# Attention scores of two layers as two stacked fp32r passes instead of one fp32 product

## The chip, the cores and the metric

The kernel runs on one NeuronCore of a Trainium2 chip. The metric is the time of one execution on the device, in microseconds; the lower the better. Before the change three runs took 4530.76, 4531.95 and 4536.92 us, median 4531.95 us. TensorE (PE) multiplies matrices, its weight loads have a row of their own (PEld); VectorE is DVE, ScalarE is ACT, GpSimd is POOL, and SP only issues DMAs.

## What is computed

One sequence of 512 tokens, width 1024, goes through two layers (a feed-forward block, a mixer of a linear recurrence and an attention with a forgetting gate, a second feed-forward block) and then through a second model part with its own mixer, memory attention and an expert layer. The change lies in the attention of the two layers:

```python
def forgetting_attention(q, k, v, f_logit, g_q, g_k):
    qn = rms_norm(q, g_q).transpose(0, 2, 1, 3)
    kn = rms_norm(k, g_k).transpose(0, 2, 1, 3)
    cum = jnp.cumsum(jax.nn.log_sigmoid(f_logit), axis=1).transpose(0, 2, 1)
    for blk in range(seq // Q_BLOCK):
        s = jnp.einsum("bhqd,bhkd->bhqk", qn[:, :, q0:q1], kn[:, :, :q1]) * HEAD_DIM ** -0.5
        s = s + cum[:, :, q0:q1, None] - cum[:, :, None, :q1]
        s = jnp.where(mask, s, -jnp.inf)
        p = jax.nn.softmax(s, axis=-1)
        outs.append(jnp.einsum("bhqk,bhkd->bhqd", p, vh[:, :, :q1]))
```

There are 16 heads of 64 features and 4 query blocks of 128 tokens; the mask is causal. Everything is float32.

## The kernel before

Features lie on the 128 partitions, tokens along the free dimension. Every weight comes as a tile of 128 x 2048 floats. ScalarE copies it to fp32r (`WH`, line 166, two halves), VectorE subtracts to get the rest (`WL`, line 174, two halves), and TensorE makes each product of three fp32r passes: high by high, high by low, low by high (`mm3`, lines 193 to 195). In what follows this is the weight split: `act_next` and `dve_next` split the tile after next.

The attention of a layer works through 8 pairs of heads. One head of a pair is on partitions 0 to 63, the other on 64 to 127. In `pe_attention` the work of three pairs is interleaved on TensorE, in an order written out by hand. While the eight steps of pair i run (2 heads by 4 query blocks, the score of block qb having 128 x (qb + 1) columns), parts of the projection of pair i + 2 fill in (`beside`); after them comes the rest of that projection (16 groups of three passes in all), and in its middle the sums, the spread and the turn for the head norm of pair i + 1 and for the output of pair i. Ahead of the last two groups stand the first two scores of pair i + 1 (`first_scores`).

A step goes: TensorE makes the score in a PSUM bank (line 1231 in plain fp32, and line 1233, which adds the causal mask by an fp32r matmul); VectorE takes the maximum (line 1035, `top`); ScalarE takes the exponential and the row sum (line 1087) and releases `p_ready`; TensorE turns the result by 128 x 128 transposes (line 993, the turn); VectorE copies that to SBUF (line 1047, `copy`); TensorE multiplies by the values (line 1003). There are three score banks, so the fourth score waits for the first exponential.

The score matmul has all 128 rows in use though a head has 64 features: `QZ[hh]` holds the normed Q of its head on its own 64 partitions, and on the other 64 the running sum of the forget gate (from `CQ`) masked by `HMASK`; `KZ[hh]` holds the normed K and there ones or the negative sums. In this way one product gives the score with both gate terms.

Between two pairs ScalarE's queue is: roots and the exponential's table, two copies of the spread norm factors (`widen`, line 1356), the high part of pair i's output (`outputs`, YH, line 1368), the weight split (line 166). VectorE's queue is: the mask products (line 1421), four norm instructions of 64 rows (two for Q, line 1425, two for K, line 1429), the low part of the output (line 1448), the weight split (line 174), and then the maxima of the next pair. The queues of an engine run strictly in program order, and every wait is on a semaphore.

Once per layer, before the attention, `dve_forget_sums` (line 1193) makes the running sums of the gate and fills `CQ` and the fixed rows of `KZ`.

Of the kernel before, what the change touches and what calls it, by code (L numbers as in the profile page):

```python
# [5 lines left out]
F32 = mybir.dt.float32  # L6
F32R = mybir.dt.float32r
# [6 lines left out]
P = 128  # L14
# [163 lines left out]
def act_next(c, act, tile, halves=(0, 1)):  # L178
    act_split(c, act, tile.t + 1, tile.next_p, tile.next_loads, halves)
# [916 lines left out]

PAIRS = HEADS // 2
JS = [(hh, qb) for hh in range(2) for qb in range(QB)]

# [93 lines left out]
def dve_forget_sums(c, dve, l):  # L1193

    V = c.nc.vector
    F = c.FW
    V.scalar_tensor_tensor(out=F[:, 0, :], in0=F[:, 4, :], scalar=-2.0, in1=F[:, 0, :], op0=ALU.mult, op1=ALU.add)
    V.memset(F[:, 2, :], 1.0)
    V.memset(c.CQ[:, :], 1.0)
    V.memset(c.KZ[0][:, :], 1.0)  # L1200
    V.memset(c.KZ[1][:, :], 1.0)
    dve.drain()
    V.tensor_tensor_scan(F[:, 1, :], F[:, 2, :], F[:, 0, :], 0.0, ALU.mult, ALU.add)
    dve.drain()
    for r in (32, 96):
        V.tensor_copy(c.CQ[r:r + 32, :], F[r:r + 32, 1, :])
    V.tensor_scalar(c.KZ[1][0:32, :], F[0:32, 1, :], -1.0, None, ALU.mult)
    V.tensor_scalar(c.KZ[0][64:96, :], F[64:96, 1, :], -1.0, None, ALU.mult)
    dve.drain()
# [14 lines left out]
def pe_attention(c, pe, cur, l):  # L1224
    base = l * PAIRS

    def steps(i, b):
        def step(hh, qb):
            def scores(S):
                nk = P * qb + P  # L1230
                c.nc.tensor.matmul(S[:, :nk], c.QZ[hh][:, qb * P:qb * P + P], c.KZ[hh][:, :nk],  # L1231
                                   start=True, stop=False)
                return c.nc.tensor.matmul(S[:, nk - P:nk], c.IDR[:, :], c.CAUSALR[:, :], start=False, stop=True)
            return {"nk": P * qb + P, "scores": scores,
                    "values": lambda kb: c.V[:, kb, bass.ds(i * P + hh * HD, HD)],
                    "out": c.PB[:, b, qb * P + hh * HD:qb * P + hh * HD + HD]}
        return Steps((base + i) * 8, [step(*x) for x in JS], (c.PM, c.PT, c.SUM), None, score_banks(b))

# [101 lines left out]
def act_attention(c, act, cur, l):  # L1340
# [25 lines left out]
    def outputs(i):  # L1366
        act.wait_ge(c.sem("ot_ready"), base + i + 1)
        c.nc.scalar.activation(c.YH[:, i, :], c.PB[:, 4, :], ACT.Copy).then_inc(c.sem("ot_hi"), 1)

    def beside(tile):  # L1370
        def work(j):
            if j == 3:
                squares(tile)
        return work
# [4 lines left out]
    exp_table()  # L1379
    widen(0)  # L1380
    act_next(c, act, Tile(cur, 0, 1, 1))
# [11 lines left out]
    exp_table()  # L1393
    widen(i + 1)
    outputs(i)
    act_next(c, act, gate)
    attend(i + 1, last.b, None)
# [8 lines left out]
def dve_attention(c, dve, cur, l):  # L1406
# [3 lines left out]
    def scale(i):  # L1410
# [4 lines left out]
                      c.R16[:, :].unsqueeze(2).to_broadcast([P, 16, HD])).then_inc(c.sem("qk_scale"), 1)  # L1415

    def norm(i, b):
        own, other = [slice(hh * HD, hh * HD + HD) for hh in range(2)], [slice(HD, P), slice(0, HD)]
        col = PRM["g_k"][0]
        for hh in range(2):  # L1420
            V.tensor_scalar(c.QZ[hh][other[hh], :], c.CQ[other[hh], :], c.HMASK[other[hh], bass.ds(i * 2 + hh, 1)],
                            None, ALU.mult)
        dve.wait_ge(c.sem("qk_wide"), (base + i) * 2 + 1)
        for hh in range(2):
            V.scalar_tensor_tensor(out=c.QZ[hh][own[hh], :], in0=c.PB[own[hh], b, :], scalar=c.GQ8[own[hh], l, 0:1],
                                   in1=c.SQ2[own[hh], 0, :], op0=ALU.mult, op1=ALU.mult)
        dve.wait_ge(c.sem("qk_wide"), (base + i) * 2 + 2)
        for hh in range(2):
            last = V.scalar_tensor_tensor(out=c.KZ[hh][own[hh], :], in0=c.PB[own[hh], b + 1, :],
                                          scalar=c.PR[own[hh], l, col:col + 1],  # L1430
                                          in1=c.SQ2[own[hh], 1, :], op0=ALU.mult, op1=ALU.mult)
        last.then_inc(c.sem("qk_ready"), 1)

# [19 lines left out]
    scale(0)  # L1453
    norm(0, first.b)
    dve_next(c, dve, Tile(cur, 0, 1, 1))
# [8 lines left out]
    norm(i + 1, last.b)  # L1464
    outputs(i)
    dve_next(c, dve, gate)
    attend(i + 1, last.b, False)
# [9 lines left out]
CONSTS = {}  # L1477
for _n, _w in (("ident", 128), ("ones", 128), ("ones_head", 128), ("causal", 128), ("head_mask", 16)):
    CONSTS[_n] = (sum(w for _, w in CONSTS.values()), _w)
# [3 lines left out]
def constants():  # L1483

    t = np.zeros((P, NCONST), np.float32)

    def put(name, a):
        at, w = CONSTS[name]
        t[:, at:at + w] = a
    i = np.arange(P)  # L1490
    put("ident", np.eye(P))
    put("ones", 1.0)
    put("ones_head", (i[:, None] // HD == i[None, :] // HD))
    put("causal", np.where(i[None, :] <= i[:, None], 0.0, NEG))
    put("head_mask", (i[:, None] % 32 == np.arange(16)[None, :]))
    return t


def allocate(c):
# [12 lines left out]
    with ExitStack() as s:  # L1512
# [4 lines left out]
    c.CT = c.sb("CT", [P, NCONST])  # L1517
    c.IDENT, c.ONES, c.ONESB, c.CAUSAL, c.HMASK = (
        c.CT[:, CONSTS[n][0]:sum(CONSTS[n])] for n in ("ident", "ones", "ones_head", "causal", "head_mask"))
    c.EPSC = c.sb("EPSC", [P, 1])  # L1520
# [6 lines left out]
    c.LW, c.RT = c.sb("LW", [P, 5, DC]), c.sb("RT", [P, QB])  # L1527
    c.sb("ALIGN", [P, 14])

# [8 lines left out]
    with ExitStack() as y:  # L1538
# [10 lines left out]
        with ExitStack() as s:  # L1549
            c.V = c.sb("V", [P, QB, D], F32, s)  # L1550
            c.CQ = c.sb("CQ", [P, S], F32, s)
            c.KZ = [c.sb(f"KZ{i}", [P, S], F32, s) for i in range(2)]
            with ExitStack() as f:
                c.FW = c.sb("FW", [P, 5, S], F32, f)
            c.QZ = [c.sb(f"QZ{i}", [P, S], F32, s) for i in range(2)]
            c.SQ2 = c.sb("SQ2", [P, 2, S], F32, s)
            c.PM, c.PT = c.sb("PM", [P, 3, S], F32, s), c.sb("PT", [P, 2, S], F32, s)
            c.OQ = c.sb("OQ", [P, QB, P], F32, s)
            c.R16, c.EXPD = c.sb("R16", [P, 16], F32, s), c.sb("EXPD", [P, 1], F32, s)
            c.RE = c.sb("RE", [P, 2, QB, P], F32, s)  # L1560
    allocate2_arena(c, stage)

# [424 lines left out]
def act_proj2(c, act, cur):  # L1987
# [18 lines left out]
    for tile in tiles(act, cur, 1):  # L2006
        act_next(c, act, tile)
        act.wait_ge(c.sem("tile_done"), tile.t + 3)
        A.activation(c.KVC[:, :, :S], c.PB[:, tile.b:tile.b + 2, :], ACT.Copy).then_inc(c.sem("ps_done"), 1)
        act.drain()  # L2010
        act.wait_ge(c.sem("kvc_pad"), 1)
        A.activation(c.KCH[:, :, :], c.KVC[:, :, :], ACT.Copy).then_inc(c.sem("cmp_hi"), 1)
# [55 lines left out]
def dve_angles(c, dve):  # L2068
    V = c.nc.vector
    T = c.T2  # L2070
    dve.wait_ge(c.sem("pos_loaded"), 16)
    V.tensor_copy(T[:, 0, :], T[:, 3, :].bitcast(I32))
# [23 lines left out]
def dve_proj2(c, dve, cur):  # L2096
# [415 lines left out]
def act_mem_raw(c, act):  # L2512

    act.wait_ge(c.sem("mem_loaded"), 16)
    act_raw(c, act, V2 + 1, c.NORM_MEM, c.MEMX, lambda k: p2(c, "memkv_g", k, 1), c.XHM, width=MEM, fresh=False)
# [897 lines left out]
def pool_second(c, pool, d):  # L3413

    pool_sum(c, pool, V2, c.NORM_MIX2, order=DOWN_ORDER)
    pool.wait_ge(c.sem("x_new"), V2 * DC + DC)
    pool.dma_start(c.T2[:, 3, :].bitcast(I32), d["positions"]).then_inc(c.sem("pos_loaded"), 16)
    pool.wait_ge(c.sem("tile_done"), T_GATES2 + 3)
# [4 lines left out]
    pool.wait_ge(c.sem("phase_done"), (PH2 + 1) * 3)  # L3423
    pool.dma_start(c.MEMX[:, :, :], d["mem"]).then_inc(c.sem("mem_loaded"), 16)
    pool_sum(c, pool, V2 + 1, c.NORM_MEM, MEM)
# [83 lines left out]
def layer_tiles(a, l):  # L3509
# [13 lines left out]
    f4 = np.zeros((D, P), f.dtype)  # L3523
    for r in (0, 32, 64, 96):
        f4[:, r:r + HEADS] = f
# [21 lines left out]
def layer_params(a, l):  # L3547
    f4 = np.zeros((P, 1), np.float32)
    for r in (0, 32, 64, 96):
        f4[r:r + HEADS, 0] = a["b_forget"][l]  # L3550
# [104 lines left out]
```

## Time and profile before

| | |
|---|---|
| median of three runs | 4531.95 us |
| profiled execution | 4530.32 us |
| its span, first to last instruction | 4528.5 us |
| TensorE busy | 4418.6 us, 98% |
| weight loads busy | 3702.0 us, 82% |
| VectorE busy | 2733.0 us, 60% |
| ScalarE busy | 1742.6 us, 38% |
| GpSimd busy | 720.8 us, 16% |
| TensorE's share of the chain that ended last | 87% |
| mean granted TensorE clock | 0.991 |

The profile is one execution. Busy time is the union of an engine's instructions; the ends of matmuls are modelled, so the distance from one start (or one weight load) to the next tells more than a duration. Attention of the first layer lies at about 636 to 860 us of the span, that of the second at about 1944 to 2170 us. A half clock means that TensorE was granted 0.50 of its full clock.

### The profile page before, as it was taken

Reading aid. Unit: us, or ns where it says so; the run is one execution under the profiler, and the core shown is the slowest. Engines: PE = TensorE matmul, PEld = TensorE weight load, DVE = VectorE, ACT = ScalarE, POOL = GpSimd, SP = SyncE. Lnnn points to the kernel's source line nnn. Section 1 sums busy time; section 2 is a strip of 40 time slices with the busy share of each in tenths; the row PEclk is TensorE's granted clock in tenths of the full one; section 3 lists DMA queues with packets and bytes.
Section 4 is the critical chain, followed back from the end, with each engine's and each line's share of the span. In section 5 each row is a group of like instructions: output and inputs, shape, how many; then the busy total and the mean of one; then the engine's idle time right before and its main releaser. Section 6 shows DMA issues by size and latency. Waiting matters only on the chain.

```text
span 4528.5 us, 61846 instructions
## 1 busy us (share of the span) xinstructions
PE 4418.6 (98%) x21997; PEld 3702.0 (82%) x21997; DVE 2733.0 (60%) x4435; ACT 1742.6 (38%) x2871; POOL 720.8 (16%) x767
## 2 busy tenths in 40 slices
PE   8999999999999999999999998899999899999999
PEld 7888888888888887888888886687667788888888
DVE  5436556454444436656454278754898877777777
ACT  3223634332232225444332233442226644444444
POOL 0000000000000000000000000010486634333332
PEclk9999999999999999999999998999999999999999
DMA  3222221122222222211222222031224688888887
GB/s 130 100 97 87 95 84 37 66 98 97 101 95 93 102 91 86 103 50 43 93 93 98 97 94 77 1 131 56 82 86 156 266 298 299 304 295 299 299 304 262
DMA packets 91046, 605.13 MB, mean 134 GB/s; under 512 B 12832, under 2 KB 13216, under 8 KB 24288
## 3 DMA queue, kind: packets, MB, share of 16 engines
q1 hardware_dynamic: 58464, 412.95, 24.8%
q0 software_dynamic: 31232, 162.29, 10.4%
q10 hardware_dynamic: 1152, 27.26, 1.4%
q8 instruction: 122, 2.00, 0.2%
q14 instruction: 76, 0.62, 0.0%
HBM read 573.10 MB, written 29.36 MB: 133 GB/s over the span
## 4 chain that ended last, share of the span: by engine, by line
PE 87%; DVE 4%; ACT 2%; issue 2%; DVEq 2%; DMA 1%; POOLq 1%; ACTq 0%; POOL 0%; SPq 0%
PE PB L193 25%; PE PB L195 24%; PE PB L194 24%; PE PB L2741 3%; PE PB L1003 2%; PE PB L1231 2%; PE PB L3030 2%; PE PB L993 1%; PE PB L3045 1%; ACT WH L3196 1%; PE PB L1244 1%; PE PB L2254 1%; POOLq L256 1%; DVE WL L3247 1%; DVE YG L3234 0%
## 5 line engine op out<-in xcount | busy, mean ns | idle before, releaser
L193 PE MATMUL PB<-XH,WH 128*128 128x512 f32 (+1 forms) x3288 | 1260.1, 383 | 21.1 <-DVE WL L174 13.6
L195 PE MATMUL PB<-XH,WL 128*128 128x512 f32 (+1 forms) x3288 | 1242.2, 378 | 0.0
L194 PE MATMUL PB<-XL,WH 128*128 128x512 f32 (+1 forms) x3288 | 1241.2, 378 | 0.0
L174 DVE TENSOR_TENSOR WL<-RAW,WH 128x1024 fp32r<-128x1024 f32 x520 | 637.3, 1267 | 480.4 <-ACT WH L166 458.7
L193 PEld LDWEIGHTS PB<-XH,WH 128*128 128x128 f32 x3288 | 619.4, 188 | 130.3 <-issue 20.9
L194 PEld LDWEIGHTS PB<-XL,WH 128*128 128x128 f32 x3288 | 619.4, 188 | 100.1 <-issue 2.2
L166 ACT ACTIVATE WH<-RAW 128x1024 fp32r<-128x1024 f32 x504 | 504.4, 1049 | 509.8 <-PE PB L195 481.7
L195 PEld LDWEIGHTS PB<-XH,WL 128*128 128x128 f32 x3288 | 618.4, 188 | 100.2
L254 POOL TENSOR_TENSOR SQ<-SQ 128x512 f32<-128x512 f32 x49 | 72.5, 1480 | 2567.8 <-ACT SQ L236 2546.1
L3247 DVE TENSOR_TENSOR WL<-RAW,WH 128x1024 fp32r<-128x1024 f32 x220 | 269.8, 1226 | 220.2 <-ACT WH L3196 219.8
L193 PE MATMUL PB<-WH,WGH 128*128 128x512 f32 x768 | 301.0, 392 | 8.4 <-DVE WGL L3263 8.4
L195 PE MATMUL PB<-WH,WGL 128*128 128x512 f32 x768 | 301.5, 393 | 0.0
L194 PE MATMUL PB<-WL,WGH 128*128 128x512 f32 x768 | 301.0, 392 | 0.0
L525 DVE TENSOR_TENSOR PB<-PB,RBF 128x512 f32<-128x512 f32 x88 | 61.6, 700 | 368.6 <-PE PB L195 368.0
L195 PE MATMUL PB<-HH,WL 128*128 (+1 forms) x704 | 273.9, 389 | 0.0
L193 PE MATMUL PB<-HH,WH 128*128 (+1 forms) x704 | 273.9, 389 | 0.0
L194 PE MATMUL PB<-HL,WH 128*128 (+1 forms) x704 | 273.9, 389 | 0.0
L501 ACT ACTIVATE SIL<-PB 128x512 f32<-128x512 f32 x88 | 52.7, 599 | 562.9 <-DVE PB L525 562.9
L3196 ACT ACTIVATE WH<-RAW 128x1024 fp32r<-128x1024 f32 x220 | 230.9, 1050 | 63.0 <-PE PB L195 60.5
L1087 ACT ACTIVATE PM<-PB,NM 128x128 f32<-128x128 f32 (+2 forms) x208 | 108.6, 523 | 245.9 <-DVE NM L1035 245.5
L193 PEld LDWEIGHTS PB<-WH,WGH 128*128 128x128 f32 x768 | 144.6, 188 | 42.8 <-issue 15.3
L3350 POOL DMA_DIRECT2D GM<-gate_matrix x128 | 114.9, 898 | 401.1 <-DVE WG L3259 371.6
(423 smaller groups left out, 7257.5 us busy)
## 6 DMA issues: line engine op xcount, KB each, us to landing
RAW<-weights SPq DMA_DIRECT2D x381, 1024.0 KB, 4.8
gate_matrix<-STG ACTq DMA_DIRECT2D x5, 4096.0 KB, 12.3
GM<-gate_matrix POOLq DMA_DIRECT2D x128, 160.0 KB, 3.3
RAW<-weights SPq DMA_DIRECT2D x12, 512.0 KB, 3.9
gate_matrix<-STG ACTq DMA_DIRECT2D x2, 2048.0 KB, 7.5
GM<-gate_matrix POOLq DMA_DIRECT2D x128, 32.0 KB, 3.7
X<-x SPq DMA_DIRECT2D x4, 512.0 KB, 8.0
x_home<-X ACTq DMA_DIRECT2D x1, 2048.0 KB, 6.9
```

The costliest lines, as they stand in the source:

```text
L166: c.nc.scalar.activation(c.WH[p][:, cols], c.RAW[p][:, cols], ACT.Copy).then_inc(c.sem("w_hi"), 1)
L174: c.nc.vector.tensor_tensor(c.WL[p][:, cols], c.RAW[p][:, cols], c.WH[p][:, cols].bitcast(F32), ALU.subtract).then_inc(c.sem("w_split"), 1)
L193: c.nc.tensor.matmul(out, wh, xh, start=start, stop=False)
L194: c.nc.tensor.matmul(out, wh, xl, start=False, stop=False)
L195: return c.nc.tensor.matmul(out, wl, xh, start=False, stop=stop)
L1003: last = c.nc.tensor.matmul(step["out"](kb) if merged else step["out"], st.PT[:w, j % 2, kb * P:kb * P + P], step["values"](kb), start=mer ...
L1087: c.nc.scalar.activation(st.PM[:, m, :nk], c.PB[:, st.banks[m], :nk], ACT.Exp, bias=c.NM[:, m:m + 1], scale=1.0, accum_out=st.SUM[:, st.su ...
L1231: c.nc.tensor.matmul(S[:, :nk], c.QZ[hh][:, qb * P:qb * P + P], c.KZ[hh][:, :nk], start=True, stop=False)
L2741: last = c.nc.tensor.matmul(c.PB[:, 6 + half, :DENSE], U[:, k, :], c.NORM_PEER.SQ[:, k, :DENSE], start=k == 0, stop=k == DC - 1)
L3196: A.activation(c.WH[p][:, cols], c.RAW[p][:, cols], ACT.Copy).then_inc(c.sem(f"h{half}_hi"), 1)
L3247: V.tensor_tensor(c.WL[p][:, cols], c.RAW[p][:, cols], c.WH[p][:, cols].bitcast(F32), ALU.subtract)\
L3350: pool.dma_start(c.GM[s][:, :whole].rearrange("p (b t) -> p b t", b=BLOCKS - 1), gm[:BLOCKS - 1, :, expert:expert + 1, :].rearrange("b p e ...
```

## The change

The product of Q and K is made of fp32r passes. The normed Q and K of a pair are first written whole to `QKN` (VectorE, two instructions of 128 rows). `QA[hh]` holds the high part of Q on the head's own 64 partitions and the low part on the other 64; `KA[hh]` holds the high part of K on both halves. Their product is Q's high plus low parts by K's high part. `QB[hh]` holds Q's high part and, on the other 64 partitions, the masked gate sums; `KB[hh]` holds the low part of K, and there the ones and negative sums. The score is then QA by KA, QB by KB, and the causal matmul. The gate sums are themselves split in a high and a low part, on alternate groups of 16 partitions (`halves`).

ScalarE makes the high parts (`high`, four copies of 64 x 512 for each head), VectorE the low ones (`low`, two subtractions for each head). Head 0's stand ahead of `outputs`, head 1's behind it, and both ahead of the weight split. The wait for `qk_ready` moves into the score, once for each head, and `qk_high` is waited for there too. The other edits are SBUF layout, constants, the gate column repeated every 16 rather than every 32 partitions, and some semaphores of the second part that are merged or dropped.

```diff
@@ dve_forget_sums
     V.memset(c.CQ[:, :], 1.0)
-    V.memset(c.KZ[0][:, :], 1.0)
-    V.memset(c.KZ[1][:, :], 1.0)
     dve.drain()
     V.tensor_tensor_scan(F[:, 1, :], F[:, 2, :], F[:, 0, :], 0.0, ALU.mult, ALU.add)
+    for hh in range(2):
+        V.tensor_copy(c.KB[hh][:, :], F[:, 2, :])
+    dve.drain()
+    V.tensor_copy(F[:, 0, :].bitcast(F32R), F[:, 1, :])
+    dve.drain()
+    V.tensor_tensor(F[:, 3, :], F[:, 1, :], F[:, 0, :], ALU.subtract)
+    dve.drain()
+    V.tensor_scalar(F[:, 3, :], F[:, 3, :], c.HALVES[:, 1:2], None, ALU.mult)
+    dve.drain()
+    V.scalar_tensor_tensor(out=F[:, 1, :], in0=F[:, 0, :], scalar=c.HALVES[:, 0:1], in1=F[:, 3, :],
+                           op0=ALU.mult, op1=ALU.add)
     dve.drain()
@@ pe_attention, scores
                 nk = P * qb + P
-                c.nc.tensor.matmul(S[:, :nk], c.QZ[hh][:, qb * P:qb * P + P], c.KZ[hh][:, :nk],
+                if qb == 0:
+                    pe.wait_ge(c.sem("qk_ready"), (base + i) * 2 + (hh + 1))
+                    pe.wait_ge(c.sem("qk_high"), (base + i) * 6 + (hh * 3 + 3))
+                c.nc.tensor.matmul(S[:, :nk], c.QA[hh][:, qb * P:qb * P + P], c.KA[hh][:, :nk],
                                    start=True, stop=False)
+                c.nc.tensor.matmul(S[:, :nk], c.QB[hh][:, qb * P:qb * P + P], c.KB[hh][:, :nk],
+                                   start=False, stop=False)
                 return c.nc.tensor.matmul(S[:, nk - P:nk], c.IDR[:, :], c.CAUSALR[:, :], start=False, stop=True)
@@ first_scores
-        pe.wait_ge(c.sem("qk_ready"), base + i + 1)
@@ act_attention
+    def high(i, hh):
+
+        if hh == 0:
+            act.wait_ge(c.sem("qk_natural"), (base + i) * 2 + 1)
+        c.nc.scalar.activation(c.QA[hh][mine[hh], :], c.QKN[mine[hh], 0, :], ACT.Copy).then_inc(c.sem("qk_high"), 1)
+        c.nc.scalar.activation(c.QB[hh][mine[hh], :], c.QKN[mine[hh], 0, :], ACT.Copy)
+        if hh == 0:
+            act.wait_ge(c.sem("qk_natural"), (base + i) * 2 + 2)
+        for rows in (mine[hh], other[hh]):
+            c.nc.scalar.activation(c.KA[hh][rows, :], c.QKN[mine[hh], 1, :], ACT.Copy).then_inc(c.sem("qk_high"), 1)
...
         widen(i + 1)
+        high(i + 1, 0)
         outputs(i)
+        high(i + 1, 1)
         act_next(c, act, ahead)
@@ dve_attention
+        for g, gain in enumerate((c.GQ8[:, l, 0:1], c.PR[:, l, col:col + 1])):
+            dve.wait_ge(c.sem("qk_wide"), (base + i) * 2 + (g + 1))
+            V.scalar_tensor_tensor(out=c.QKN[:, g, :], in0=c.PB[:, b + g, :], scalar=gain, in1=c.SQ2[:, g, :],
+                                   op0=ALU.mult, op1=ALU.mult).then_inc(c.sem("qk_natural"), 1)
+        dve.drain()
+
+    def low(i, hh):
+
+        dve.wait_ge(c.sem("qk_high"), (base + i) * 6 + (hh * 3 + 1))
+        V.tensor_tensor(c.QA[hh][other[hh], :], c.QKN[mine[hh], 0, :], c.QA[hh][mine[hh], :].bitcast(F32), ALU.subtract)
+        dve.wait_ge(c.sem("qk_high"), (base + i) * 6 + (hh * 3 + 2))
+        V.tensor_tensor(c.KB[hh][mine[hh], :], c.QKN[mine[hh], 1, :], c.KA[hh][mine[hh], :].bitcast(F32), ALU.subtract)\
+            .then_inc(c.sem("qk_ready"), 1)
...
         attend(i, own.b)
         norm(i + 1, after.b)
+        low(i + 1, 0)
         outputs(i)
+        low(i + 1, 1)
         dve_next(c, dve, ahead)
```

For the first pair of a layer there is no output to make; `high(0, 0)`, `high(0, 1)` and `low(0, 0)`, `low(0, 1)` stand between the norm and the weight split.

## Rows read from the trace of the kernel before

**Rows 1.** The page: busy us, share of the span and instructions of each engine.

```profile
PE 4418.6 (98%) x21997; PEld 3702.0 (82%) x21997; DVE 2733.0 (60%) x4435; ACT 1742.6 (38%) x2871; POOL 720.8 (16%) x767
```

**Rows 2.** Timeline (start us, length us, engine, line, operation), weight loads of scores.

```profile
781.40 0.30 PEld L1231 LDWEIGHTS PB<-KZ,QZ 128*128 128x128 f32 x2
...
782.38 0.20 PEld L993 LDWEIGHTS PB<-CT,PM 128*128 128x128 f32 x2 [0.24 <-issue]
...
648.06 0.32 PEld L1231 LDWEIGHTS PB<-KZ,QZ 128*128 128x128 f32 x2
648.30 0.19 PEld L1233 LDWEIGHTS PB<-CAUSALR,IDR 128*128 128x128 f32 x1
648.41 0.30 PEld L1231 LDWEIGHTS PB<-KZ,QZ 128*128 128x128 f32 x2
...
648.95 0.19 PEld L193 LDWEIGHTS PB<-XH,WH 128*128 128x128 f32 x1
```

**Rows 3.** Timeline, neighbouring fp32r passes of 512 and of 256 columns.

```profile
777.99 0.39 PE L194 MATMUL PB<-XL,WH 128*128 128x512 f32 x1
778.22 0.39 PE L195 MATMUL PB<-XH,WL 128*128 128x512 f32 x1
...
377.15 0.28 PE L193 MATMUL PB<-WH,XH 128*128 128x256 f32 x1
377.27 0.28 PE L194 MATMUL PB<-WL,XH 128*128 128x256 f32 x1
```

**Rows 4.** Timeline of one boundary between pairs: ScalarE, VectorE, and the turn.

```profile
772.03 1.09 ACT L1356 ACTIVATE SQ<-PB 128x512 f32<-128x512 f32 x2 [3.27 <-PE PB L1254]
773.76 2.00 ACT L166 ACTIVATE WH<-RAW 128x1024 fp32r<-128x1024 f32 x2
...
772.66 1.52 DVE L1425 SCALAR_TENSOR_TENSOR QZ<-PB,GQ,SQ 64x512 f32<-64x512 f32 x2 [0.55 <-ACT SQ L1356]
776.35 2.35 DVE L174 TENSOR_TENSOR WL<-RAW,WH 128x1024 fp32r<-128x1024 f32 x2
778.92 0.29 DVE L1035 TENSOR_REDUCE NM<-PB 128x1 f32<-128x128 f32 x1 [0.23 <-PE PB L1233]
...
781.34 0.14 PEld L993 LDWEIGHTS PB<-CT,PM 128*128 128x128 f32 x1
```

**Rows 5.** An SBUF copy with its follower (timeline); 512-column subtractions (groups by form).

```profile
106.98 0.63 ACT L503 ACTIVATE HH<-PROD 128x512 f32 x1 [1.01 <-DVE PROD L529]
107.51 1.99 ACT L166 ACTIVATE WH<-RAW 128x1024 fp32r<-128x1024 f32 x2
...
L531 DVE TENSOR_TENSOR HL<-PROD,HH 128x512 f32 x80 | 55.4, 693 | 74.6 <-ACT HH L503 74.6
```

**Rows 6.** Timeline, pair 0 of the first layer: split, first exponential, first turn.

```profile
645.22 2.01 ACT L166 ACTIVATE WH<-RAW 128x1024 fp32r<-128x1024 f32 x2
...
650.68 0.37 ACT L1087 ACTIVATE PM<-PB,NM 128x128 f32<-128x128 f32 x1 [3.45 <-DVE NM L1035]
...
651.26 0.14 PEld L993 LDWEIGHTS PB<-CT,PM 128*128 128x128 f32 x1 [0.30 <-issue]
```

**Rows 7.** Timeline, VectorE behind the forget sums of the first layer.

```profile
613.72 1.22 DVE L890 TENSOR_TENSOR M<-PB,AA 128x1024 f32<-128x1024 f32 x1 [1.54 <-PE PB L195]
```

**Rows 8.** TensorE gaps (timeline); stretches behind them: busy us, third-last granted clock.

```profile
464.91 0.50 PE L193 MATMUL PB<-YH,WH 128*128 128x512 f32 x1 [2.80 <-ACT PB L681]
465.80:469.20 3.40, 3.40 (x10) 2.62 (x9) 1.38 (x2) 1.45 (x3) 0.00 (x0) 0.50 0.63 265
...
2822.25 0.66 PE L993 MATMUL PB<-CT,PM 128*128 128x128 f32 x4 [1.36 <-ACT PM L1087]
2824.40:2831.20 6.80, 6.80 (x25) 5.28 (x25) 5.88 (x14) 1.26 (x5) 0.00 (x0) 0.50 0.00 0
...
2807.58 0.66 PE L993 MATMUL PB<-CT,PM 128*128 128x128 f32 x4 [1.56 <-ACT PM L1087]
2807.50:2811.00 3.50, 3.42 (x26) 2.94 (x26) 3.01 (x8) 1.08 (x4) 0.00 (x0) 1.00 0.00 0
```

More of the change, by code:

```diff
@@ L1380, in act_attention @@
     widen(0)
+    for hh in range(2):
+        high(0, hh)
     act_next(c, act, Tile(cur, 0, 1, 1))
@@ L1415, in scale @@
                       c.R16[:, :].unsqueeze(2).to_broadcast([P, 16, HD])).then_inc(c.sem("qk_scale"), 1)
+    mine, other = HALF_ROWS, HALF_ROWS[::-1]
     def norm(i, b):
-        own, other = [slice(hh * HD, hh * HD + HD) for hh in range(2)], [slice(HD, P), slice(0, HD)]
         col = PRM["g_k"][0]
         for hh in range(2):
-            V.tensor_scalar(c.QZ[hh][other[hh], :], c.CQ[other[hh], :], c.HMASK[other[hh], bass.ds(i * 2 + hh, 1)],
+            V.tensor_scalar(c.QB[hh][other[hh], :], c.CQ[other[hh], :], c.HMASK[other[hh], bass.ds(i * 2 + hh, 1)],
                             None, ALU.mult)
[L1423 to L1432, printed above, removed]
+        for g, gain in enumerate((c.GQ8[:, l, 0:1], c.PR[:, l, col:col + 1])):
[9 more added lines that the diff above has]
+            .then_inc(c.sem("qk_ready"), 1)
     def attend(i, b, ahead=True):
@@ L1454, in dve_attention @@
     norm(0, first.b)
+    for hh in range(2):
+        low(0, hh)
     dve_next(c, dve, Tile(cur, 0, 1, 1))
@@ L1464, in dve_attention @@
     norm(i + 1, last.b)
+    low(i + 1, 0)
     outputs(i)
+    low(i + 1, 1)
     dve_next(c, dve, gate)
@@ L1477 @@
 CONSTS = {}
-for _n, _w in (("ident", 128), ("ones", 128), ("ones_head", 128), ("causal", 128), ("head_mask", 16)):
+for _n, _w in (("ident", 128), ("ones", 128), ("ones_head", 128), ("causal", 128), ("head_mask", 16), ("halves", 2)):
     CONSTS[_n] = (sum(w for _, w in CONSTS.values()), _w)
@@ L1494, in constants @@
     put("causal", np.where(i[None, :] <= i[:, None], 0.0, NEG))
-    put("head_mask", (i[:, None] % 32 == np.arange(16)[None, :]))
+    put("head_mask", (i[:, None] % HEADS == np.arange(HEADS)[None, :]))
+    put("halves", (i[:, None] // HEADS % 2 == np.arange(2)[None, :]))
     return t
@@ L1517, in allocate @@
     c.CT = c.sb("CT", [P, NCONST])
-    c.IDENT, c.ONES, c.ONESB, c.CAUSAL, c.HMASK = (
-        c.CT[:, CONSTS[n][0]:sum(CONSTS[n])] for n in ("ident", "ones", "ones_head", "causal", "head_mask"))
+    c.IDENT, c.ONES, c.ONESB, c.CAUSAL, c.HMASK, c.HALVES = (
+        c.CT[:, CONSTS[n][0]:sum(CONSTS[n])] for n in ("ident", "ones", "ones_head", "causal", "head_mask", "halves"))
     c.EPSC = c.sb("EPSC", [P, 1])
@@ L1551, in allocate @@
             c.CQ = c.sb("CQ", [P, S], F32, s)
[L1552 removed]
+            c.KB = [c.sb(f"KB{i}", [P, S], F32R, s) for i in range(2)]
             with ExitStack() as f:
                 c.FW = c.sb("FW", [P, 5, S], F32, f)
[L1555 removed]
+            c.PM, c.PT = c.sb("PM", [P, 3, S], F32, s), c.sb("PT", [P, 2, S], F32, s)
+            c.QA, c.KA, c.QB = ([c.sb(f"{n}{i}", [P, S], F32R, s) for i in range(2)] for n in ("QA", "KA", "QB"))
             c.SQ2 = c.sb("SQ2", [P, 2, S], F32, s)
[L1557 removed]
             c.OQ = c.sb("OQ", [P, QB, P], F32, s)
@@ L1560, in allocate @@
             c.RE = c.sb("RE", [P, 2, QB, P], F32, s)
+            c.QKN = c.RE[:, :, :, :].rearrange("p g q d -> p g (q d)")
     allocate2_arena(c, stage)
@@ L3523, in layer_tiles @@
     f4 = np.zeros((D, P), f.dtype)
-    for r in (0, 32, 64, 96):
+    for r in range(0, P, HEADS):
         f4[:, r:r + HEADS] = f
@@ L3548, in layer_params @@
     f4 = np.zeros((P, 1), np.float32)
-    for r in (0, 32, 64, 96):
+    for r in range(0, P, HEADS):
         f4[r:r + HEADS, 0] = a["b_forget"][l]
```

21 lines of the change are left out of this document (12 added, 9 removed).

## The prediction

> **What bounds the kernel now.** I read the page's busy shares first: TensorE is busy for 98% of the span and no other engine is above 60% [rows 1]. A microsecond of matmul work removed is then a microsecond of span, provided that TensorE doesn't end up waiting for somebody in its place. So the question is where, in the stage that the change touches, the three engines meet. That stage is the attention of both layers, 16 pairs of heads in all. The first turn of pair 0 starts at 651.26 [rows 6], that of pair 5 at 781.34 [rows 4]: 26.0 us a pair. The second view is the timeline of that boundary between two pairs [rows 4]: the reader is to see that VectorE does the second half of its weight split, and immediately after it the first maximum of the next pair (778.92, after a wait of 0.23 us for the scores). VectorE is thus at that place already as late as it may be, while ScalarE is done with its split at 775.76 (773.76 + 2.00). TensorE reaches the first turn of the new pair (the transposes of line 993) at 781.34 and isn't held there.
>
> **What the faster scores give.** Of TensorE I count from weight load to weight load, since ends of matmuls are modelled. A 512-column score in plain fp32, with its causal matmul, holds TensorE from 781.40 to 782.38, 0.98 us; a 256-column one from 648.41 to 648.95, 0.54 us; a 128-column one from 648.06 to 648.41, 0.35 us [rows 2]. In fp32r one 512-column pass takes 0.23 us and one of 256 columns 0.12 us, start to start [rows 3]; a load whose matmul is short costs 0.11 us (648.30 to 648.41) [rows 2]. The new score is two such passes and the causal one: 2 x 0.23 + 0.11 = 0.57 us at 512 columns, 2 x 0.12 + 0.11 = 0.35 at 256, and three loads, 0.33, at 128. The gains are 0.41, 0.19 and nothing; the 384-column score lies between, 0.30. A head gains 0.90 us, a pair 1.80, the 16 pairs **28.8 us**.
>
> **What is put on ScalarE and VectorE.** Per pair, ScalarE gets eight copies of 64 x 512. The nearest row is a copy from SBUF to fp32r of 512 columns: 0.63 us long, the next instruction 0.53 us after its start [rows 5]. I charge 0.53, since 64 partitions rather than 128 gain nothing in the old norm (0.76 us for each 64-row instruction, 1.52 for two [rows 4]). Bounds: 0.50 (the two PSUM copies at 772.03, 1.09 us together with the last one's tail) and 0.57. VectorE loses two of its four norm instructions (the two new ones do 128 rows each, 0.75 us) and gets four subtractions of 0.69 us [rows 5].
>
> **The boundary walked with these.** All times are those of rows 4.
> - Copies to SQ2 start at 772.03; the norm of Q at 772.66, so QKN's Q is there at 773.41 and its K at 774.17.
> - ScalarE, from 773.45: four copies to 775.57, then YH (0.50) to 776.07, four copies to 778.19. Only now the weight split, which before began at 773.76: 4.4 us later.
> - VectorE's own four subtractions fit in the gaps between these copies, and the low part of head 0 is ready at about 775.9 (KA's first copy ends 775.14, then 0.69), before TensorE wants it at 778.22. So the first scores don't wait.
> - ScalarE's first split half ends at about 779.24 (half of 2.00 us and some tail); VectorE's two halves take 2.35 us from 779.28, to 781.63. Behind them are queued, on VectorE, the maxima of the next pair: 781.66 to 781.95. ScalarE's exponential waits for the maximum, TensorE's turn for the exponential. From the exponential's start to the load of the turn it took 0.58 us in the pair where TensorE was waiting for it (650.68 to 651.26) [rows 6]. So the turn starts at 781.95 + 0.04 + 0.58 = 782.57, against 781.34 before: **1.23 us later**.
> - The scores before the turn gave 0.19 + 0.30, so TensorE stands for 1.23 + 0.49 = 1.7 us there. The scores after it (512, 128, 256, 384, 512 columns) still give 1.31. The pair's net is 1.23 - 1.31 = -0.08 us.
>
> That holds for 14 of the 16 pairs: **-1.1 us**. The gain of 28.8 us is, almost to the last microsecond, spent in a new wait. I find no second new wait in the eight steps: maxima and exponentials start as soon as their scores are there, and these come earlier by as much as TensorE does.
>
> **The first pair of each layer** has no YH, but its copies for both heads stand ahead of the split. ScalarE was free for the split at 645.22 [rows 6]. By the same offsets (773.45 is 0.43 after ScalarE's widening copies leave it free) the copies run from 645.65 to 649.89, the splits of VectorE from 650.98 to 653.33, the maximum to 653.65, the turn starts at 654.27. It was 651.26, so 3.01 us later, with 1.31 given back: +1.7 us, twice: **+3.4 us**. TensorE stands there for about 3.5 us. A gap of 2.80 us (464.91) was followed by 3.4 us at half clock (granted 0.50, the level of 1.2 GHz) [rows 8]. I take the clock to fall in both of these pairs; 3.4 us at half costs 1.7 us where TensorE works throughout, and part of that stretch it waits for the softmax, so 1.5 each: **+3.0 us**. Bounds 0 and 3.4.
>
> **Edits with one answer.** The forget sums get some 2.5 us more of VectorE work per layer (two clears out, five whole-width operations of 0.5 to 0.75 in). Behind them VectorE waited 1.54 us for TensorE at 613.72 [rows 7], so the gated output there comes about 1 us later; TensorE takes that bank up only a tile (48 passes of 0.23 us) later. Nothing. The SBUF layout, two more columns of constants, repeated forget columns and merged semaphores of the second part: nothing; the events waited for are older than the waits. No DMA is added; the load of the next weight tile waits for a split that comes 3 us later, with a pair of 26 us to land in.
>
> **Sum.** The profiled execution took 4530.32 us. 4530.3 - 1.1 + 3.4 + 3.0 = 4535.6. The median of the runs is 1.6 above it: **4537 us**. Unknown prices around this: a copy at 0.50 or 0.57 moves each boundary by 8 x 0.03, over 16 pairs -4 or +5; the clock -3; a few hundredths per score +-3. Its own range is 4528 to 4546.
>
> **Rivals.**
> - *The clock falls at ordinary boundaries too (slower).* A gap of 1.36 us at 2822.25 was followed by a stretch of 6.8 us at 0.50, one of 1.56 us at 2807.58 by a stretch at 1.00 [rows 8]. TensorE's new wait of 1.7 us is longer than both. For it: the first row. Against: work is dense before each boundary here, while around 2822 TensorE waited again and again. Each fall costs about 1.5 us as above; at all 14 boundaries 21 us, 4558. From a third of them, with 7 us, it is slower than can be called the same. 21%.
> - *The copies are hidden (faster).* Were a 64-row copy half as long, 8 x 0.27 = 2.1 us less, the maximum would be no later than before, no wait would come in, and all but a little of 28.8 us would stay: 4508. The 64-row norm at 0.76 us speaks against it. 6%.
> - *The fp32r passes of the scores are no faster than fp32* (the change doesn't do what it says). Then each pair is 1.23 later, the first ones 3.0, and the clock: 17 + 6 + 3 = 26 us, 4558. The projections of the same shape speak against it. 4%.
> - *Shorter weight loads.* If an fp32r load took half of 0.11 us, the five scores after the turn would gain another 0.17 + 4 x 0.055 = 0.39 us a pair, 6 us in all: 4531. The causal load is an fp32r one and took 0.11 [rows 2], so I give it 2%. This is what the Trainium skill says (TensorE: Matmul & The Clock Gate, Weight-path perf modes): Fast Weight Load is on for 128 weights whose type is not fp32, at about twice the speed. This trace's fp32r loads don't show it.
>
> **How the numbers follow.** The forecast has the remaining 67%. What a measurement of this kernel can tell from no change is 0.2%, 9 us: 4523 to 4541. Faster: the 6% and a little of the forecast's lower end, 0.08. Slower: the clock rival and the fp32 one, and the upper end of the forecast, 0.32. Same: 0.60. The range leaves out 4508 and the far end of the clock's case: 4524 to 4556.
>
> **What would show it.** In the profile after: score passes of 0.23 us start to start; ScalarE's weight split beginning about 4.4 us later behind eight copies; TensorE idle 1.4 to 2 us before the first line-993 transpose of each pair, ended by ScalarE's exponential, and about 3.5 us in pairs 0; a pair still taking 26 us; granted clock 0.50 for 3.4 us in each first pair. I am wrong if that idle time is under 1 us (then faster), or if the clock stays low after it (then slower).

## The result, and the profile after the change

The changed kernel takes 4567.09 us (median of 6 runs, 4565.06 to 4568.46), beside 4532.3 us for the kernel before in the same session (6 runs). The ratio is 1.0079 with a 95% interval of 1.0068 to 1.0089: 35 us slower, four times what a measurement of this kernel can tell from no change. I had predicted 4537 with a range up to 4556. The profiled execution took 4568.25 us, its span is 4566.1 us (4528.5 before).

The head of the page of after, and its shares of the chain that ended last, answer to [rows 1]:

```profile
span 4566.1 us, 62194 instructions
PE 4421.6 (97%) x21997; PEld 3724.3 (82%) x21997; DVE 2754.5 (60%) x4475; ACT 1815.3 (40%) x2999; POOL 726.9 (16%) x767
...
PE 84%; DVE 5%; ACT 4%; issue 4%; DVEq 2%; POOLq 1%; DMA 0%; ACTq 0%; POOL 0%; SPq 0%
```

TensorE's busy time is no lower than before (4421.6 us against 4418.6), though the scores became cheaper. Matmuls take longer at a lower clock (a 512-column score pass is 0.40 us long at 712.60, at full clock, and 0.63 at 793.27, at half), so this row is the first sign that the clock fell. The second view is the windows of the kernel before between the same three pairs of marks (the 2850th and 3300th projection matmul, the 8100th and 8700th, the 11250th and 11400th): the attention of layer 1, the attention of layer 2, and the attention in the kernel's second part, which the change doesn't touch. Columns: busy us and count of PE, PEld, DVE, ACT, POOL, then granted clock, DMA share, GB/s.

```profile
634.50:858.90 224.40, 223.58 (x1348) 188.19 (x1348) 129.65 (x235) 105.87 (x217) 0.00 (x0) 1.00 0.12 42
1919.20:2178.20 259.00, 257.81 (x1498) 216.23 (x1497) 140.38 (x247) 113.03 (x225) 0.00 (x0) 1.00 0.14 49
2753.80:2985.00 231.20, 198.85 (x1442) 161.02 (x1442) 170.41 (x329) 92.31 (x221) 9.46 (x16) 0.91 0.12 41
```

The same windows of after:

```profile
631.90:872.40 240.50, 222.64 (x1348) 197.83 (x1347) 138.99 (x251) 141.85 (x281) 0.00 (x0) 0.94 0.11 40
1934.10:2207.30 273.20, 254.93 (x1497) 223.98 (x1497) 151.77 (x266) 148.96 (x289) 0.00 (x0) 0.96 0.13 47
2782.90:3022.10 239.20, 207.52 (x1442) 167.27 (x1440) 170.35 (x329) 92.59 (x221) 9.49 (x16) 0.87 0.11 40
```

The two attentions that were changed take 16.1 and 14.2 us more, **30.3 us**, and their granted clock is 0.94 and 0.96, where it was 1.00. The third row is a surprise: code that is the same in both kernels takes 8.0 us more, at a clock of 0.87 instead of 0.91. All else between the marks differs by 3 us at most. 30.3 + 8.0 and some -0.8 for the rest make the 37.6 us between the spans (the sums in this document are of marks that weren't rounded).

Third view: timeline of one boundary between pairs in after, which answers to [rows 4]. Columns: start us, length us, engine, line, operation, and in brackets the idle time before and what ended it.

```profile
701.18 1.09 ACT L1370 ACTIVATE SQ<-PB 128x512 f32<-128x512 f32 x2 [3.27 <-PE PB L1269]
702.60 0.63 ACT L1390 ACTIVATE QA<-RE 64x512 fp32r<-64x512 f32 x1 [0.33 <-DVE RE L1459]
703.14 0.62 ACT L1391 ACTIVATE QB<-RE 64x512 fp32r<-64x512 f32 x1
703.66 1.27 ACT L1395 ACTIVATE KA<-RE 64x512 fp32r<-64x512 f32 x2
704.95 0.60 ACT L1382 ACTIVATE YH<-PB 128x512 f32 x1
705.58 0.63 ACT L1390 ACTIVATE QA<-RE 64x512 fp32r<-64x512 f32 x1
...
707.92 2.01 ACT L166 ACTIVATE WH<-RAW 128x1024 fp32r<-128x1024 f32 x2
...
709.01 2.36 DVE L174 TENSOR_TENSOR WL<-RAW,WH 128x1024 fp32r<-128x1024 f32 x2 [1.05 <-ACT WH L166]
711.29 1.08 DVE L1035 TENSOR_REDUCE NM<-PB 128x1 f32<-128x128 f32 x3
...
711.61 0.37 ACT L1087 ACTIVATE PM<-PB,NM 128x128 f32<-128x128 f32 x1 [1.68 <-DVE NM L1035]
...
712.20 0.32 PE L993 MATMUL PB<-CT,PM 128*128 128x128 f32 x1 [1.97 <-ACT PM L1087]
```

This is the chain that the prediction walked: eight copies, the split behind them, VectorE's half of the split, the maximum, the exponential, the turn, with TensorE standing in front of it. The split starts 6.74 us behind the start of the copies to SQ2 (701.18 to 707.92; before 1.73 us, [rows 4]). TensorE stands for 1.97 us (1.89 to 1.98 in all 14 pairs that aren't the first of a layer; I call these the ordinary pairs), where I had worked out 1.7.

What I had got wrong stands in the fourth view, the windows of after between the first scores of neighbouring pairs (pairs 1 to 6 of layer 1; before, a pair took 26.0 us and its clock was 1.00 throughout):

```profile
678.40:707.70 29.30, 27.39 (x163) 24.83 (x161) 17.13 (x32) 16.90 (x35) 0.00 (x0) 0.88 0.10 36
707.70:734.10 26.40, 24.40 (x162) 21.58 (x161) 16.87 (x32) 16.71 (x35) 0.00 (x0) 1.00 0.10 40
734.10:760.60 26.50, 24.57 (x163) 21.74 (x162) 17.04 (x32) 16.88 (x35) 0.00 (x0) 1.00 0.11 40
760.60:788.30 27.70, 25.73 (x163) 23.13 (x161) 17.07 (x32) 16.83 (x35) 0.00 (x0) 0.94 0.10 38
788.30:816.00 27.70, 25.81 (x163) 23.14 (x162) 17.15 (x32) 16.91 (x35) 0.00 (x0) 0.94 0.11 38
816.00:842.40 26.40, 24.40 (x163) 21.59 (x161) 16.88 (x32) 16.71 (x35) 0.00 (x0) 1.00 0.12 42
```

The pairs come in three lengths: 26.4 us where the clock stays, 27.7 us where it is at half speed for 3.4 us, 29.3 us where it is for 6.8 us. Two such stretches of half clock, behind the turn of pair 4 (which started at 765.05) and in the first pair, where TensorE had waited for 3.7 us:

```profile
765.70:769.00 3.30, 3.30 (x18) 3.29 (x17) 1.87 (x5) 2.28 (x7) 0.00 (x0) 0.50 0.76 295
...
652.90:663.20 10.30, 10.30 (x48) 9.98 (x47) 4.72 (x10) 3.95 (x11) 0.00 (x0) 0.50 0.22 91
```

TensorE does 18 matmuls in the first of them; in a stretch of the same length behind the turn of pair 2, at full clock, it did 27. In both layers together 8 of the 14 ordinary pairs have such a stretch: six of 3.4 us and two of 6.8. I had expected it in the first pairs alone.

### The profile page after: what moved, and what is told of

Read it like the earlier page. It is cut to its first block, busy times and chain, and to the rows that moved or that the text cites. A ratio compares the mean times of both kernels' runs of the same rounds, so it can differ in the third digit from the quotient of the medians.

```text
span 4566.1 us, 62194 instructions
## 1 busy us (share of the span) xinstructions
PE 4421.6 (97%) x21997; PEld 3724.3 (82%) x21997; DVE 2754.5 (60%) x4475; ACT 1815.3 (40%) x2999; POOL 726.9 (16%) x767
## 3 DMA queue, kind: packets, MB, share of 16 engines
q0 software_dynamic: 31232, 162.29, 10.2%
## 4 chain that ended last, share of the span: by engine, by line
PE 84%; DVE 5%; ACT 4%; issue 4%; DVEq 2%; POOLq 1%; DMA 0%; ACTq 0%; POOL 0%; SPq 0%
PE PB L193 24%; PE PB L195 23%; PE PB L194 23%; PE PB L2785 3%; PE PB L1003 3%; PE PB L3074 2%; PE PB L993 2%; PE PB L3089 1%; ACT WH L3240 1%; ACT KA L1395 1%; ACT WH L166 1%; PE PB L2298 1%; PE PB L1259 1%; DVE WL L174 1%; DVE WL L3291 1%
## 6 DMA issues: line engine op xcount, KB each, us to landing
gate_matrix<-STG ACTq DMA_DIRECT2D x5, 4096.0 KB, 12.4
```

## The experiments

**Theory A**, formed on this trace: the time is lost in TensorE's new wait ahead of each pair's first turn, once as the wait, and once more because the granted clock falls behind it in about half of the pairs. **Theory B**: the low clock accompanies the slower boundaries without costing much, and the loss lies in the longer chain of ScalarE and VectorE alone. **Theory C** is on the 8 us of the second part: they depend on where the steps of the clock happen to fall in an execution, and not on the change; by **Theory D** the change causes them.

**Filling the wait.** Seven matmuls that nobody reads, ahead of the first turn of each pair. They change neither the chain of ScalarE and VectorE nor the moment at which the turn may start; they only keep TensorE at work.

```diff
     for j in range(2 if begun else 0, st.depth):
         pe_scores(c, pe, st, j)
+    if fill:
+        fill()
     turn(0)
...
+    def fill():
+        for n in range(7):
+            c.nc.tensor.matmul(c.PB[:, 5, :], c.IDR[:, :], c.XH[:, n, :], start=True, stop=True)
```

> The changed kernel with seven more fp32r matmuls of 512 columns (identity by XH, into the unused bank 5, 7 x 0.23 = 1.6 us) put on TensorE ahead of the first turn of each pair, where it now waits 1.9 us. They compute nothing that is used. Theory A (the clock): the new waits cost 0.4 us a pair by themselves, and the rest of the loss comes from the half clock that follows them (51 us at 0.50 in the two attentions of the profile after). Then the added work makes the kernel faster: no stretch at half clock in ordinary pairs, 15 to 20 us less, 4547 to 4552. Theory B (the queues alone: the half clock hits work that would wait anyway, and the loss is all in ScalarE's and VectorE's longer chains): the time stays at 4567 or gets longer.

Measured: 4545.78 us, 1.0035 of before [1.0023 to 1.0046]; span 4547.1. That is 21 us less than the changed kernel took, for work that does nothing, and 1 us below the range that A gave. (The two were measured in different sessions. Each against the kernel before beside it, the change costs 34.8 us and the change with the wait filled 16.1: 19 us less.) Windows of two ordinary pairs, and the timeline of TensorE at the boundary:

```profile
676.80:703.20 26.40, 26.15 (x170) 22.88 (x169) 16.96 (x32) 16.79 (x35) 0.00 (x0) 1.00 0.12 40
703.20:729.60 26.40, 26.08 (x170) 22.81 (x168) 16.88 (x32) 16.72 (x35) 0.00 (x0) 1.00 0.11 40
...
705.55 1.85 PE L1291 MATMUL PB<-XH,IDR 128*128 128x512 f32 x7
707.68 0.33 PE L993 MATMUL PB<-CT,PM 128*128 128x128 f32 x1 [0.28 <-ACT PM L1089]
```

All 14 ordinary pairs now take 26.4 us, at full clock. The period is the one that after's undisturbed pairs have, so the chain is unchanged and only the clock is different: A, not B. In the profiles the attentions of both layers take 18 us less than in after. The first pairs take 29.5 and 29.6 us; each still has 3.4 us of half clock, and TensorE still stands for 2.04 us there, since seven matmuls don't fill that wait. The attentions of both layers are still 12.4 us above before.

**The wait without the change.** The kernel before, with eight idle copies of 64 x 512 (each followed by a drain) on ScalarE ahead of the weight split, and nothing else changed.

```diff
+    def idle_copies():
+        for n in range(8):
+            c.nc.scalar.activation(c.JK[0:HD, :], c.CQ[0:HD, :], ACT.Copy)
+            act.drain()
...
         widen(i + 1)
         outputs(i)
+        idle_copies()
         act_next(c, act, ahead)
```

> The kernel before, with its plain fp32 scores, and eight copies of 64 x 512 (into a buffer that nobody reads, each drained) on ScalarE ahead of each weight split of the pairs: the wait of the change without its gain. By the queues the first turn comes 1.7 us later in 14 pairs and 3 us in 2, so 30 us. Theory A: to that comes the half clock, as in the changed kernel, 15 to 20 us: 4578 to 4582. Theory B: 4562.

Measured: 4581.51 us, 1.0115 [1.0098 to 1.0132]. Two neighbouring pairs and the turn:

```profile
709.40:739.10 29.70, 27.60 (x164) 23.43 (x162) 15.96 (x29) 17.23 (x35) 0.00 (x0) 0.94 0.09 36
739.10:767.40 28.30, 26.15 (x162) 21.92 (x161) 15.78 (x29) 17.18 (x34) 0.00 (x0) 1.00 0.11 37
...
714.52 0.33 PE L993 MATMUL PB<-CT,PM 128*128 128x128 f32 x1 [2.10 <-ACT PM L1087]
```

With the plain fp32 scores in place, a wait of 2.1 us again puts the clock at half speed for 3.4 us, here in every second pair, and again such a pair is 1.3 to 1.4 us longer. The fall thus belongs to the wait and not to the fp32r passes, the new layout or the subtractions. That the time came out inside A's 4578 to 4582 is luck: the fall came in 6 of 14 ordinary pairs, and the next experiment puts it at 9 us where I had expected 15 to 20, while the longer queues cost 43 where I had expected 30.

**The same wait, filled.** The kernel with idle copies and the seven matmuls of the first experiment.

> The same with the seven unused matmuls of e1_fill ahead of each first turn. Theory A: the half clock goes, 4562 to 4566. Theory B: the same as e2_wait, both at 4562.

Measured: 4572.8 us, 1.0097 [1.008 to 1.0114], 7 us above what A gave. One ordinary pair:

```profile
705.80:734.10 28.30, 27.83 (x170) 23.20 (x169) 15.78 (x29) 17.21 (x34) 0.00 (x0) 1.00 0.11 37
```

No ordinary pair has half clock any more, and all take 28.3 us: that part of A holds. My number was wrong, since I had put the undisturbed pair with idle copies at 27.7 us and it takes 28.3. Filling saved 9 us here and 19 to 21 in the changed kernel, in keeping with fewer stretches of half clock to begin with (17.1 and 13.7 us in the two attentions, against 27.3 and 23.9).

**The gain alone.** The kernel before with Q and K held as fp32r and two fp32r passes for each score, without any high and low parts. It leaves out the low parts of Q and K, and with them the copies and subtractions, and adds the same product twice, so it stands for the price of two passes only.

```diff
                 c.nc.tensor.matmul(S[:, :nk], c.QZ[hh][:, qb * P:qb * P + P], c.KZ[hh][:, :nk],
                                    start=True, stop=False)
+                c.nc.tensor.matmul(S[:, :nk], c.QZ[hh][:, qb * P:qb * P + P], c.KZ[hh][:, :nk],
+                                   start=False, stop=False)
...
-            c.KZ = [c.sb(f"KZ{i}", [P, S], F32, s) for i in range(2)]
+            c.KZ = [c.sb(f"KZ{i}", [P, S], F32R, s) for i in range(2)]
```

> The gain alone: the kernel before, with QZ and KZ written as fp32r and each score made of two fp32r passes of the same QZ by KZ. It leaves out the low parts and with them all copies and subtractions (and adds the same product twice). The queues of ScalarE and VectorE are those of before. My sum gave 28.8 us for the passes: 4503 to 4505. If the passes are worth less than counted, or the softmax chain takes over as the bound within the eight steps, it is 4510 or more.

Measured: 4506.74 us, 0.9949 [0.9932 to 0.9965].

```profile
694.98:719.31 24.33, 24.25 (x163) 21.64 (x162) 15.97 (x30) 12.27 (x26) 0.00 (x0) 1.00 0.12 43
```

A pair takes 24.33 us instead of 26.02: the cheaper scores give 1.69 us a pair, 26.3 us over both attentions. So the gain is real, and nearly what I had counted (1.80 and 28.8). In this profile the second part, unchanged, took 7.1 us more than before, which is why the span falls by 21 us only.

**The split first.** The changed kernel with the weight split moved ahead of head 1's four copies on ScalarE, and ahead of its two subtractions on VectorE.

```diff
         high(i + 1, 0)
         outputs(i)
-        high(i + 1, 1)
         act_next(c, act, ahead)
+        high(i + 1, 1)
...
         low(i + 1, 0)
         outputs(i)
-        low(i + 1, 1)
         dve_next(c, dve, ahead)
+        low(i + 1, 1)
```

> The changed kernel with one thing moved: on ScalarE and on VectorE the weight split stands ahead of head 1's copies and subtractions (which are needed only by the fifth score of the pair) instead of behind them. The first maximum comes about 1 us earlier, so TensorE's wait before the first turn falls from 1.9 to about 1 us. If the wait is what costs (theory A), a pair takes 25.4 us instead of 26.4, and no ordinary pair sees the half clock any more: 4520 to 4530, faster than the kernel before or equal to it. If the clock falls all the same, 4540 or more. If the place of the copies in the queue doesn't matter (theory B: the chains' length does), nothing changes from 4567.

Measured: 4531.61 us beside 4531.58 for before, 1.0001 [0.9992 to 1.0011]. An ordinary pair and its turn:

```profile
700.80:726.30 25.50, 24.44 (x163) 21.62 (x161) 17.13 (x33) 16.63 (x35) 0.00 (x0) 1.00 0.11 41
...
704.35 0.32 PE L993 MATMUL PB<-CT,PM 128*128 128x128 f32 x1 [1.03 <-ACT PM L1087]
```

The pair has the length that I expected (25.4), the wait has shrunk to 1.03 us, and no ordinary pair in either layer has half clock. The order of the two queues is worth 33 us, with the same instructions (4564.51 for the change as made on the same chip, below). The total came out 1.6 us above the expected 4520 to 4530. The first pairs still wait for 2.92 us; in the profile that of the second layer is followed by 13.7 us of half clock, that of the first layer by none. But the profiled execution took 4539.78 us, 8 above the median, so its stretches aren't those of a typical one; what keeps the median above 4530 isn't shown.

**The copies out of the way.** The two copies of head 1 that its subtractions need stay between the split and the first exponential; the other two go behind the second exponential, and both subtractions behind the second maximum. VectorE's own chain to the first maximum then has nothing of head 1 in it.

```diff
     for j in range(st.depth):
         top(j)
+        if early and j == 1:
+            early()
     copy(0)
...
         def work(j):
-            if j == 3:
+            if j == 1:
+                high_rest()
+            if tile and j == 3:
                 squares(tile)
...
         act_next(c, act, ahead)
+        high_first(i + 1)
```

> The changed kernel with head 1's work taken apart: ScalarE makes its two copies for the subtractions between the weight split and the first exponential, and the other two behind the second exponential; VectorE does the two subtractions behind the second maximum, where it waits for TensorE. By the queues the first turn waits for nothing, and the fifth score for about 0.4 us. A pair should take 24.3 (as with the gain alone) to 24.8 us, no half clock in ordinary pairs: 4507 to 4515, faster than both kernels. If a new wait comes in at the fifth score that is longer than 1 us, 4520 or more.

Measured: 4519.18 us (11 runs, 4517.05 to 4529.48), 0.9976 [0.9967 to 0.9985]. This one beats both kernels: 12 us faster than before (4531.58 beside it) and 45 faster than the change as made, on the same chip (4564.51, below).

```profile
703.79:728.71 24.92, 24.23 (x163) 21.63 (x162) 17.15 (x33) 16.87 (x35) 0.00 (x0) 1.00 0.12 42
...
704.90 0.62 DVE L1035 TENSOR_REDUCE NM<-PB 128x1 f32<-128x128 f32 x2
705.55 0.69 DVE L1480 TENSOR_TENSOR QA<-RE,QA 64x512 fp32r<-64x512 f32 x1
706.25 0.69 DVE L1482 TENSOR_TENSOR KB<-RE,KA 64x512 fp32r<-64x512 f32 x1
706.97 0.56 DVE L1035 TENSOR_REDUCE NM<-PB 128x1 f32<-128x384 f32 x1
```

The turn of an ordinary pair no longer waits. The pair's 24.92 us are still 0.6 above the 24.33 of the gain alone, and the timeline shows what I take for the reason: the maximum of the third score stands behind the two subtractions, and everything after it is late by as much. Instead of that one wait TensorE now has short ones, 0.7 us at most in ordinary pairs, for the transposed probabilities that VectorE copies (9 times, 5.2 us from 670 to 870). Whether a different place for the second subtraction would recover the rest wasn't tried. The median is 4 us above the expected end. In the profile the first pairs take 29.7 and 26.8 us, and the first had 6.8 us of half clock; but this is the slowest of the 11 executions (4529.48 us). They fall into two groups, eight at 4517.05 to 4519.93 us with a mean granted clock of 0.991 or 0.992, and three at 4527.60 to 4529.48 with 0.988 or 0.989, of which the profiled one is one.

**The changed kernel again**, unaltered, in a later session, on the chip of the two kernels above.

> The changed kernel once more, unaltered. In its profile the attention of the second part (whose instructions the change leaves alone) took 239.2 us with 61 us at half clock, against 231.1 us with 41 in the profile before; e1_fill and e4_gain have 239 and 238 too, e2_wait and e3_wait_fill 230 and 231. Theory C: this is a matter of where the chip's clock steps fall against that stage in the execution that was profiled, and another profile of the same kernel can show 231. Theory D: the change does it, and it is 239 again. The two attentions of the layers: 240 and 273 us between the same marks again, within 5 us.

Measured: 4564.51 us, 1.0076 [1.006 to 1.0091]. The third of the windows:

```profile
2783.60:3018.50 234.90, 202.83 (x1442) 163.96 (x1441) 170.39 (x329) 92.58 (x221) 9.46 (x16) 0.89 0.12 40
```

The attentions took 240.8 and 276.2 us, as in the first profile within 3 us, so their loss repeats; half clock came in 6 of the 14 ordinary pairs, not all of them the same ones as in the first profile (pair 4 had 6.8 us instead of 3.4, pair 5 none instead of 3.4). The second part took 234.9 us here and 239.2 in the first profile of the same program, with 51 and 61 us of half clock. Over the nine profiles it took 230 to 231 us in three, 235 in one and 238 to 239 in five, whatever had been changed ahead of it, and always less where there was less half clock. Something of it is then set by chance, which speaks for C.

For D speaks that the three at 230 to 231 are just the kernels with plain fp32 scores, and the six at 235 to 239 those with two passes. The runs of the kernel with the copies out of the way bear on this, since they differ by 10 us without any change. The clock is granted at 0.50 or 1.00, so twice what the mean clock lacks to 1, times the span, is the time at half clock: 105 us in its profile, 61 of them in the second part. In its two runs with a mean of 0.992 (4517.05 and 4519.18 us) it is 72 us, at most 77 by the rounding. No profile of the nine has less than 31 us outside the second part, so at most 46 were left for it there; the profiles at 230 to 235 have 38 to 51. By this estimate a kernel with two-pass scores is also found near the lower values, in executions that weren't profiled, and D in its strict form, 239 us each time, is out. Why the nine profiles cluster as they do stays open.

## Why the prediction was wrong, step by step

- **The boundary between pairs: right in kind, too small in size.** The wait came in where I had put it, ended by the exponential, behind the maximum, VectorE's split, ScalarE's split and the eight copies. The term that was mis-sized is the copies. I charged 0.53 us each; from the first to the split it took 5.32 us (702.60 to 707.92, with YH among them), where my walk had 4.74 us (773.45 to 778.19). From one start to the next it is 0.52 to 0.54 us where the next copy reads and writes the same 64 partitions, which I had right, and 0.62 to 0.66 where either differs: the copy into the other half of KA, YH and WH (all 128 partitions) behind KA, QA behind YH. This holds at all 16 boundaries, with a semaphore wait in between or without; the cause wasn't looked for. The load of the turn came 1.70 us later than before, measured from the start of the copies to SQ2 (11.01 us against 9.31), where I had 1.23.
- **What is given back behind the turn: right.** A pair of after without half clock takes 26.42 us, 0.40 more than before; 1.70 later less 1.31 given back is just that. I had predicted -0.08. Over 14 pairs this is +5.7 us where I had -1.1.
- **The gain of a pair:** 1.69 us against my 1.80, from the kernel that has the gain alone. Right within 6%.
- **The clock at ordinary boundaries: this is the step that failed.** I gave it 21%, with 4558 us, as a rival, and argued that work is dense ahead of each boundary, and that a wait of 1.56 us had left the clock alone while one of 1.36 had not [rows 8]. It fell in 8 of 14 ordinary pairs. From the lengths of the pairs, six times 1.3 us and two times 2.9, it cost 13.6 us, and I had put the forecast on zero. The dense work ahead of the wait didn't protect these 8. The prediction's own sign of this case, a clock that stays low behind the wait, is what the profile shows. Two observations were in any case too thin to weigh a price that falls 14 times; and the wait turned out as 1.97, well outside both. My price for a fall of 3.4 us was near: 1.3, where I had 1.5. The reason that I gave for it, that TensorE waits for the softmax in part of the stretch, isn't borne out: TensorE is idle for 1.97 us in a pair with the fall (27.70 less 25.73) and for 2.00 in one without (26.40 less 24.40), so all of the 1.3 us is busy time.
- **The first pair of each layer:** they are 6.5 and 4.6 us longer than before (32.7 and 30.8 us against 26.2), where I had 1.7 + 1.5 each. The kernel with filled waits, at 29.5 us with 3.4 us of half clock, puts the part without the clock at 2.0; I had 1.7. The rest is the clock again: 10.2 and 6.8 us of half clock in place of the 3.4 that I took from the row of the wait of 2.80 us. Both together are 11.1 us instead of 6.4.
- **Sum of the two attentions:** 5.7 + 13.6 + 11.1 = 30.4 us, against 30.3 between the marks. My terms for the same were -1.1 + 0 + 6.4 = 5.3.
- **The second part:** I put it at nothing, and the profile has 8.0 us there. No term of the change belongs to it; it would have been right to widen the range by this much. It is also the part of the loss that I can't assign.
- **What took the time out of the range:** no term alone. The forecast with the 13.6 us of the ordinary pairs would be 4551, still below 4556. Against my sum the clock is 17.7 us more in all 16 pairs (13.6, and some 4 in the first pairs), the chain at the boundaries 7.4 us, and the second part 8.0. The rival's own 4558 for a fall at all 14 boundaries was too low too, since it left out the other two.
- **The other rivals.** Copies of 64 rows are not half as long: they take 0.63 us. The fp32r passes are faster, by 1.69 us a pair. The fp32r weight loads are not shorter: in the timeline of after's weight loads, those of the two score passes and of the causal one follow each other by 0.11 us, the same as the causal load of [rows 2]. The Trainium skill (TensorE: Matmul & The Clock Gate, Weight-path perf modes) has the faster load on for 128 weights that are not fp32. The fp32r loads show none of it here: each is 0.19 us long, and the plain fp32 loads of line 1231 in before have the same 0.19.

```profile
713.23 0.19 PEld L1244 LDWEIGHTS PB<-KA,QA 128*128 128x128 f32 x1
713.34 0.19 PEld L1246 LDWEIGHTS PB<-KB,QB 128*128 128x128 f32 x1
713.45 0.19 PEld L1248 LDWEIGHTS PB<-CAUSALR,IDR 128*128 128x128 f32 x1
```

- **The edits with one answer:** the stages around the forget sums, and all between the marks outside the attentions, are unchanged within 1 to 3 us.

The mechanism of the boundary, the sign and the place were in the prediction; it was decided by a cost that follows such a wait in about half of the cases, taken at zero for 14 waits because one longer than the shortest had been harmless.

## What to carry to other kernels

A wait that is put on TensorE in a loop costs more than its length: work out how long it becomes, and if rows of the same kernel show the clock falling behind a wait of that size even once, charge the fall at each boundary for a share of the cases, not at none. Work that a faster step makes necessary on other engines belongs behind whatever TensorE waits for next: with the same instructions, the order of the queues moved this change from 33 us slower than before to 12 us faster. Where such a wait can't be removed, matmuls that nobody reads can be cheaper than standing still, as they were in both kernels here. And the profile is one execution: before its stretches are used to explain a median, its time belongs beside the times of the other runs.

## What the runs showed of the hardware

- A wait of 1.9 to 2.1 us of TensorE was followed by a granted clock of 0.50, the level of 1.2 GHz, for 3.4 or 6.8 us in 8 of 14 ordinary pairs of after (6 in its second profile), and for 3.4 us in every second one (6 of 14) of the kernel with idle copies. Where the wait of ordinary pairs was 0.94 to 1.03 us (split first) or 0.2 to 0.5 us of it were left (the two kernels with the wait filled), none of 14 had it. The length alone doesn't decide: of the two first pairs with a wait of 1.38 us (copies out of the way) one was followed by 6.8 us of half clock and one by none, and of those with 2.92 us (split first) one by 13.7 us and one by none. A stretch of 3.4 us cost 1.3 us, one of 6.8 us 2.9 us, less than the 1.7 and 3.4 of work at half speed throughout: in 3.3 us of such a stretch TensorE did 18 matmuls in place of 27, two thirds.
- Seven matmuls of 512 columns for nothing, ahead of each pair's first turn, made the changed kernel 19 to 21 us faster (4567.09 to 4545.78; the kernel before took 4532.3 and 4529.7 beside them).
- A copy of 64 x 512 from SBUF to fp32r takes ScalarE as long as one of 128 x 512: 0.63 us. The next one starts 0.52 to 0.54 us after it where it reads and writes the same 64 partitions, and 0.62 to 0.66 where either differs (in after QA to QB 0.54, the first copy of KA to the one into its other half 0.64).
- The same instructions of the kernel's second part took 230 to 239 us between the same marks, by how much of them ran at half clock (38 to 61 us).
